# Last attention of a two-layer decoder trunk: heads of two branches taken by turns, and GpSimd's block split moved ahead of the branch sums

## The reference

```python
def mixer_nsa_moba(h, w_in, ..., w_out, rel_table):
    ...
    o_cmp, p_cmp = nsa_compressed(qc, kc, vc, ...)
    sel_idx = nsa_select(p_cmp, S)
    o_slc = nsa_selected(qc, ks, vs, sel_idx, c_cols)            # 8 heads, selected blocks
    o_win = band_attention(qc, kw, vw, NSA_WINDOW, c_cols)       # 8 heads, sliding window of 256
    g = jax.nn.sigmoid(gl).reshape(B, S, 3, C_KV_HEADS, G, 1)
    o_c = g[:, :, 0] * o_cmp + g[:, :, 1] * o_slc + g[:, :, 2] * o_win
    o_d = moba_attention(qd, kd, vd, rel_table[...])             # 8 heads, last branch
    o = jnp.concatenate([o_c, o_d], axis=-1)
    return o @ w_out                                             # 256x1024 by 1024x1024
```

## Time and profile before

| what | value |
|---|---|
| median of 3 runs | 964.48 us (964.38 to 964.98) |
| profiled execution | 964.63 us |
| its span, first to last instruction | 962.9 us |
| TensorE matmul busy | 955.8 us, 99% of the span |
| VectorE busy | 775.8 us, 81% |
| ScalarE busy | 498.6 us, 52% |
| GpSimd busy | 120.9 us, 13% |
| granted TensorE clock | 0.999 of full speed |

### The profile page before, as it was taken

One profiled execution on the slowest core, in us unless ns is written; L12 is line 12 of the kernel. 1 busy time (PEld: TensorE's weight loads), 2 busy tenths in 40 slices (PEclk: granted clock), 3 DMA queues, 4 the chain that ended last, 5 costly groups with the idle time before them and its releaser, 6 DMA issues.

```text
span 962.9 us, 13459 instructions
## 1 busy us (share of the span) xinstructions
PE 955.8 (99%) x4668; PEld 808.6 (84%) x4668; DVE 775.8 (81%) x1470; ACT 498.6 (52%) x806; POOL 120.9 (13%) x129
## 2 busy tenths in 40 slices
PE   9999999999999999999999999999999999999997
PEld 7888888899888888888888888888889888888886
DVE  6889888768578988887898888878788588888884
ACT  7434443678464443445635353567677455343432
POOL 1200000166520000000200000022243420000000
PEclk9999999999999999999999999999999999999999
DMA  9976566242755657477084756527740436665631
GB/s 354 317 239 211 182 224 217 66 145 87 242 196 175 230 167 250 140 240 236 25 299 164 236 172 221 218 88 226 259 166 11 154 110 216 222 216 176 204 102 44
DMA packets 122323, 179.20 MB, mean 186 GB/s; under 512 B 3073, under 2 KB 97433, under 8 KB 122021
## 3 DMA queue, kind: packets, MB, share of 16 engines
q1 hardware_dynamic: 118900, 172.39, 53.5%
q10 hardware_dynamic: 3072, 5.11, 1.6%
q0 software_dynamic: 304, 1.09, 0.3%
HBM read 177.49 MB, written 1.09 MB: 185 GB/s over the span
## 4 chain that ended last, share of the span: by engine, by line
PE 97%; DVE 1%; issue 1%; ACT 0%; DMA 0%; POOL 0%; DVEq 0%; POOLq 0%
PE ps L1350 93%; PE ps L1616 1%; PE ps L1391 1%; PE ps L1364 0%; PE ps L1752 0%; DMA lead<-in_first 0%; DVE w_lo L1891 0%; DVE end_hi L2199 0%; PE ps L1476 0%; DVE down_lo L2190 0%; DVE logit L2071 0%; ACT logit L1142 0%; DVE probt L2085 0%; DVE xn L2205 0%; DVE x L1945 0%
## 5 line engine op out<-in xcount | busy, mean ns | idle before, releaser
L1350 PE MATMUL ps<-w_hi,xt_hi 128*128 128x512 f32 (+4 forms) x914 | 351.4, 388 | 0.5 <-ACT w_hi L982 0.5
L1350 PE MATMUL ps<-w_hi,xt_lo 128*128 128x512 f32 (+3 forms) x912 | 348.6, 385 | 0.0
L1350 PE MATMUL ps<-w_lo,xt_hi 128*128 128x512 f32 (+3 forms) x912 | 348.5, 385 | 0.0
L1891 DVE TENSOR_TENSOR w_lo<-raw,w_hi 128x2048 fp32r<-128x2048 f32 (+3 forms) x107 | 234.9, 2234 | 47.5 <-ACT w_hi L945 47.0
L1991 DVE STREAM_TRANSPOSE ps<-h 32x128 f32<-32x128 f32 x624 | 201.4, 323 | 9.2
L945 ACT ACTIVATE w_hi<-raw 128x2048 fp32r<-128x2048 f32 (+3 forms) x110 | 200.0, 1865 | 1.8 <-PE ps L1350 1.6
L1350 PEld LDWEIGHTS ps<-w_hi,xt_lo 128*128 128x128 f32 x912 | 171.1, 188 | 33.4
L1350 PEld LDWEIGHTS ps<-w_hi,xt_hi 128*128 128x128 f32 x914 | 171.3, 188 | 33.1 <-issue 0.7
L1350 PEld LDWEIGHTS ps<-w_lo,xt_hi 128*128 128x128 f32 x912 | 171.2, 188 | 32.7 <-DVE w_lo L1905 0.3
L1060 ACT ACTIVATE ht_hi<-ps 128x512 fp32r<-128x512 f32 x40 | 23.9, 598 | 284.1 <-DVE ps L1991 283.1
L1350 PE MATMUL ps<-down_hi,ht_hi 128*128 128x512 f32 x320 | 124.9, 390 | 0.0
(11 more groups left out here) (220 smaller groups left out, 841.8 us busy)
## 6 DMA issues: line engine op xcount, KB each, us to landing
raw<-in_l_ffn_wg SPq DMA_DIRECT2D x41, 1024.0 KB, 7.3
raw<-in_l_ffn_wu SPq DMA_DIRECT2D x41, 1024.0 KB, 9.8
raw_down<-in_l_ffn_wd SPq DMA_DIRECT2D x40, 1024.0 KB, 5.0
raw<-in_l_w_in SPq DMA_DIRECT2D x10, 1024.0 KB, 6.9
raw<-in_l_w_out SPq DMA_DIRECT2D x8, 1024.0 KB, 6.1
xn<-in_l_ffn_wd SPq DMA_DIRECT2D x4, 1024.0 KB, 7.2
raw<-in_l_w_in SPq DMA_DIRECT2D x4, 768.0 KB, 6.3
lead<-in_first SPq DMA_DIRECT2D x7, 384.0 KB, 6.0
```

What stands on the lines that cost most here:

```text
L1350: return pe.matmul(dst, lhs, rhs, start=start, stop=stop, skip_group_check=True)
L1891: dve.tensor_tensor(part(w_lo), part(raw), part(w_hi).bitcast(F32), ALU.subtract).then_inc(main_lo, 1)
```

## The change

The order of the steps changes: the eight heads of win1 (256 keys) and the eight of moba0 (128 keys) stand by turns, win1 head 0, moba0 head 0, win1 head 1, and so on. In these 16 steps ACT copies the probabilities of units 0, 3 and 6 of every eight, where it copied 0 and 2. DVE takes the shares of win1 and moba0 together, two steps behind the last of them, and scales win1 at step 37 and moba0 at step 39 of the pipeline. GpSimd makes the high parts and the first low part of block n0+9 ahead of the first branch sum, adds slc0 and win0, makes the second low part, and adds slc1 and win1.

```diff
-    LAST_STEPS = (("slc", "win", 0), ("slc", 1), ("win", 1), ("moba", 0), ("moba", 1))
-    ALL_STEPS = LAST_BASE + HEADS * len(LAST_STEPS)
+    LAST_STEPS = ([(("slc", 0, hh), ("win", 0, hh)) for hh in range(HEADS)] + [(("slc", 1, hh),) for hh in range(HEADS)] +
+                  [((name, t, hh),) for hh in range(HEADS) for name, t in (("win", 1), ("moba", 0))] +
+                  [(("moba", 1, hh),) for hh in range(HEADS)])
+    ALL_STEPS = LAST_BASE + len(LAST_STEPS)
...
         def copied_by_act(u):
 
-            return u // UNITS != ATT["mla"] and u % HEADS in (0, 2)
+            by_turns = LAST_BASE + 2 * HEADS <= u < LAST_BASE + 4 * HEADS
+            return u // UNITS != ATT["mla"] and u % HEADS in ((0, 3, 6) if by_turns else (0, 2))
...
-            def split_low(n):
-
-                pool.wait_ge(main_lo, 2 * n)
-                for i, part in enumerate(pieces(n)):
+            def split_low(n, which=(0, 1)):
+
+                for i in which:
+                    part = pieces(n)[i]
+                    pool.wait_ge(main_lo, 2 * n + i)
                     pool.wait_ge(main_hi, 2 * n + 1 + i)
                     pool.tensor_tensor(part(w_lo), part(raw), part(w_hi).bitcast(F32), ALU.subtract).then_inc(main_lo, 1)
 
-            def split_both(n):
+            def make_high(n):
...
+            def split_both(n):
+                make_high(n)
                 split_low(n)
 
-            def add_branches():
-                for i, (name, t) in enumerate((("slc", 0), ("win", 0), ("slc", 1), ("win", 1))):
+            def add_branches(first, end):
+                for i in range(first, end):
+                    name, t = (("slc", 0), ("win", 0), ("slc", 1), ("win", 1))[i]
...
-                    add_branches()
-                    split_both(first_block["l1_mix"] + len(MIX1_BLOCKS) + 1)
+                    n = first_block["l1_mix"] + len(MIX1_BLOCKS) + 1
+                    make_high(n)
+                    split_low(n, which=(0,))
+                    add_branches(0, 2)
+                    split_low(n, which=(1,))
+                    add_branches(2, 4)
...
+            def shares_of_next():
+
+                dve.wait_ge(probs_ready, units_by(last_step("moba", 0)))
+                both, gated = slice(column("win", 1, 0), column("moba", 0, HEADS)), columns("win", 1)
+                link(dve.reciprocal(share[:, both], total[:, both]))
+                link(dve.tensor_tensor(share[:, gated], share[:, gated], gate[:, 1, 2 * HEADS:3 * HEADS], ALU.mult))
...
-                 24: lambda: shares_of("win", 1, gate_no=2), 32: lambda: shares_of("moba", 0), 40: lambda: shares_of("moba", 1)},
+                 32: shares_of_next, 40: lambda: shares_of("moba", 1)},
                 {8: lambda: scale_branch(0, "slc", 0), 10: lambda: scale_branch(1, "win", 0),
-                 16: lambda: scale_branch(2, "slc", 1), 24: lambda: scale_branch(3, "win", 1),
-                 32: lambda: scale("moba", 0, 512), 40: lambda: scale("moba", 1, 512)}, turned="out1")
+                 16: lambda: scale_branch(2, "slc", 1), 32: lambda: scale_branch(3, "win", 1),
+                 34: lambda: scale("moba", 0, 512), 40: lambda: scale("moba", 1, 512)}, turned="out1")
```

More of the change, by code:

```diff
@@ L343, in parts_of @@
                 return ((("swa", "mla")[u // UNITS], u % UNITS // HEADS, u % HEADS),)
-            *names, t = LAST_STEPS[(u - LAST_BASE) // HEADS]
-            return tuple((name, t, u % HEADS) for name in names)
+            return LAST_STEPS[u - LAST_BASE]
         def width_of(u):
```

## The result

The changed kernel takes 976.59 us (median of 5 runs, 971.27 to 980.26), the kernel before beside it 964.47 us (964.33 to 964.98). The ratio is 1.0122, with an interval of 1.0101 to 1.0142: slower by 12 us. 969.0 was predicted, with a range of 964.1 to 970.6. The profiled execution is the shortest of the five: 971.27 us with a span of 969.5, 6.6 us over the span before. TensorE's mean granted clock in it is 0.995 of full speed; in the other four it is 0.983 to 0.990, and they take 976.3 to 980.3 us.

A forecast was written before the change was run, and what follows sets the result against it. TensorE, busy 955.8 of 962.9 us, was taken as the bound. Holds of 1.9 + 2.9 less 0.3 for the reordering give +4.5: span 967.4, execution 969.1, median 969.0 us, range 964.1 to 970.6.

The forecast's parts named there:

- Where the bound lies, and the slack: TensorE bounds; DVE's late copies stall it, by each hold (2.7, 3.7 us) less 0.8 us of slack: 1.9 and 2.9.
- Where GpSimd's work lands: Block n0+9's high parts run from 720.3, its low parts from 724.0 and, after win0's sum, from 734.1 us.
- That a multiplication with two SBUF operands is held to the end of a GpSimd instruction: DVE's multiplications by gates wait for GpSimd's 4.55 us low parts to end: holds of 2.7 and 3.7 us.
- The sum of the gaps: TensorE's two stalls in the last attention, behind DVE's held multiplications: 1.9 and 2.9 us.
- The reordering at -0.3: Wide and narrow heads by turns remove TensorE's gaps in the moba0 steps: 0.3 us gained, bounds 0 and 0.3.
- The slack for scales and copies: DVE has a fifth or more spare in the paired steps, covering 0.43 us of shares and 0.6 of a scale.
- The move of GpSimd's block is worth nothing: Splitting block n0+9 earlier gains 0: TensorE needs it only at about 758 or later, and nothing was late.
- Rival 1: No hold, also if the first low part began after 725.9, letting both multiplications pass: 964.2 us, chance 0.22.
- Rival 2: Only one hold, the second multiplication preceding the second low part, 0.9 us away: +1.6, 966.1 us; chance 0.09.
- rival 3: Holds cost more: TensorE's clock may fall to 1.2 GHz, or no slack: 6.4 us, 970.6 and more; chance 0.04.
- The likeliest case: Both multiplications held, 1.9 + 2.9 - 0.3 = +4.5 us: own range 967.5 to 970.4 us, chance 0.65.

The follow-up runs named there:

- vector_late_little: after_in_order plus one DVE memset of 0.64 us ahead of each of the two multiplications by gates: 964.87 us, ratio 1.0000 to the kernel before.
- after_in_order: Changed kernel, but GpSimd waits for DVE's first multiplication by gates before its first low part and the second before its second: 964.56 us, ratio 0.9996.
- order_only: Changed kernel with the heads by turns, but GpSimd splits the second block behind all four sums as in the kernel before: 965.29 us, ratio 1.0005.
- second_hold_only: Changed kernel, but GpSimd waits for DVE's first multiplication by gates before its first low part, with no second wait: 964.43 us, ratio 0.9995.
- first_hold_only: Changed kernel, but GpSimd waits for DVE's second multiplication by gates before its second low part, with no first wait: 966.17 us, ratio 1.0022.
- change_again: The changed kernel itself, unaltered and run once more, heads by turns: 976.58 us, ratio 1.0115 to the kernel before.
- change_copies_before: Changed kernel with heads by turns, but ACT copies units 0 and 2 of every eight throughout, as before: 978.12 us, ratio 1.0123.
- change_in_rows: Changed kernel, but win1's eight heads stand in a row and moba0's eight behind them: 970.03 us, ratio 1.0057.
- gpsimd_only_again: Repeat of gpsimd_only, the kernel before with GpSimd's new order alone and heads in rows: 969.62 us, ratio 1.0083.
- change_third: The changed kernel itself, unaltered, in another repeat with heads by turns: 976.52 us, ratio 1.0130 to the kernel before.
- gpsimd_only: The kernel before with GpSimd's new order alone, the order of heads as before: 969.20 us, ratio 1.0049.
- vector_late: after_in_order plus plain DVE memsets ahead of the two multiplications by gates, planned as 2.6 and 3.8 us: 978.35 us, ratio 1.0132.
- gaps_filled_right: Changed kernel with 7 and 12 TensorE matmuls of zeros in its two gaps, ahead of the scores of units 14 and 22: 968.71 us, ratio 1.0038.

## Why the prediction was wrong, point by point

- **Where the bound lies, and the slack**: right. The copies of probabilities ended both gaps. A hold of 2.68 cost TensorE 1.74 us (predicted 1.9), one of 3.86 cost 2.79 (predicted 2.9); that is 0.94 and 1.07 less, for a predicted slack of 0.8. With DVE late by 0.86 and 0.85 us in vector_late_little, TensorE lost 0.24 in all.
- **Where GpSimd's work lands**: right. High parts from 719.76 (predicted 720.3), low parts from 723.46 (724.0) and 733.57 (734.1); the half microsecond is the earlier end of block n0+7.
- **That a multiplication with two SBUF operands is held to the end of a GpSimd instruction**: right, and shown from three sides (operand, length, order). The largest meeting in the trace before was of 2.4 us; here one GpSimd instruction of 4.5 us held as fully. The Trainium skill's rule of a lock held for the whole instruction ("SBUF — State Buffer", section "SBUF: two separate sides") agrees with 2.68 and 3.86 us here.
- **The sum of the gaps**: 4.8 predicted, 4.5 measured. With the clock held up by fillers the kernel takes 968.7 us, against 969.0 predicted: without the clock the forecast would have come out.
- **The reordering at -0.3**: right. The medians can't tell it from nothing (after_in_order 0.9996, interval 0.9987 to 1.0005), but the traces of five kernels without long holds have 30.34 or 30.35 us from block n0+7's last product to the turning of `attn`, against 30.66. The slack for scales and copies was there: in after_in_order no gap shows.
- **The move of GpSimd's block is worth nothing**: right for the old order of heads only. In the new order win1's sum comes late, and without the move TensorE waits 0.5 us for the last low part (order_only).
- **Rival 1, by timing**: second_hold_only is that case. A first low part behind the first multiplication makes the second pass too: 964.43 (964.2 worked out). **Rival 2**: first_hold_only, 966.17 (966.1 worked out). The changed kernel was 0.69 us from it (0.9 predicted).
- **The step that failed** is in rival 3. It names the lower clock while TensorE stands for 2 to 3 us, bounds it by a step that would last up to twice as long, and then gives it no price and, at 0.04, almost no chance. The likeliest case's sum has no term for it. That term measured 3.0 us in the shortest of the first five runs and about 8 in the median. The row for it was at hand: a step of 0.90 us could last 1.80, so each step at the lower level costs up to 0.90, and a stretch of eight steps 7 us. What no row gave was how long such a stretch lasts, and an unknown like that belongs into the range and not out of it.

What stays open is why the stretch at 1.2 GHz lasts about 3.5 us in the profiles with the heads in rows and in others, by turns, 17 and 27 us, while TensorE is busy in both, and what decides in which run it falls behind the first gap. None of the runs tells that apart; ACT's copies are excluded.

None of the kernels beats the one before: the best ratios (0.9995 to 0.9997) all have 1 in their intervals. The order of the heads can be had without loss when GpSimd waits for the multiplications.

## What to carry to other kernels

Before long GpSimd instructions are moved, list DVE's operations with two SBUF operands in the new stretch: even one of 8 columns stops DVE's whole queue until the GpSimd instruction ends. Put the small one in front, give it one operand from PSUM, or cut the long one. And when waits make TensorE stand, price the work behind them at the lower clock too: here 1.55 us idle was enough in some executions, the stall was 4.5 us in all and the bill 12. Filling such a gap with matmuls of zeros brought most of it back, but removing the wait brought all.

## What the runs showed of the hardware

- A multiplication with two SBUF operands was held, one with a single SBUF operand was not: 128x16 and 128x8 multiplications took 2.68 and 3.86 us against a GpSimd instruction of 4.5 us, and 0.17 us inside one when the reciprocal was in PSUM. Reciprocals, which read one SBUF operand, kept 0.24 and 0.19 us inside the same GpSimd instructions.
- The hold is for one instruction at a time: with four instructions of 1.25 us it was 0.64 and 0.57 us.
- TensorE standing for 1.55 us (idle) was followed by 1.2 GHz in the profiles of change_again, change_copies_before, change_in_rows and gpsimd_only_again, and not in those of the changed kernel, change_third, gpsimd_only and first_hold_only. A stretch at 1.2 GHz lasted from about 3.5 us to about 31 (vector_late), and could be long with TensorE busy all through: 20.00 of 20.00 us at 0.50 in change_copies_before.
- Matmuls of zeros kept the clock at 1.00: in gaps_filled_right as many records as filled 1.73 and 2.84 us were enough.
